# A streaming-encoder layer with a gathered expert stage on one core: the opening's fillers cut into single products, half of tile 1's top-64 moved among the first dots, tile 1's first attention steps moved four picks later

## The reference

```python
h = rmsnorm(x, ln1_g)
q_a, k_a, v_a, q_i, k_i, w_i, q_b, k_b, v_b, g_b = project(h, w_in)
dots = einsum('bthd,bsd->bths', q_i, k_i)                       # indexer
score = einsum('bth,bths->bts', w_i, relu(dots))
top_s, idx = lax.top_k(score, topk)                              # 64 of the prompt's keys
p = softmax(q . k_sel[idx] * 64 ** -0.5); o_a = p @ v_sel[idx]   # sparse attention, 8 heads
o_b, S = retention_mix(q_b, k_b, v_b, g_b, ...)                  # chunked retention, 4 heads
x = x + concat([o_a, o_b]) @ w_out
h2 = rmsnorm(x, ln2_g)                                           # then the experts:
q = h2 @ w_query; s1, s2 = q . keys1, q . keys2                  # 8 heads, 2 halves, 128 keys each
e_idx, gate = top 16 of the 16 x 16 sums of the two top-16s, softmax
x = x + sum_k gate_k * gelu(exp_u[e_idx_k] . h2) * exp_v[e_idx_k]
y = rmsnorm_final(x)
```

## Time and profile before

| | |
|---|---|
| median of 3 runs | 1145.2 us (1144.81 to 1145.22) |
| profiled execution: time, span | 1146.64 us, 1144.6 us |
| PE, PEld busy | 865.9 us (76%), 398.9 us (35%) |
| DVE, ACT, POOL busy | 784.9 us (69%), 453.8 us (40%), 538.3 us (47%) |
| DMA | 456.58 MB, 399 GB/s mean over the span |

### The profile page before, as it was taken

The page is one execution under the profiler, slowest core; times in us unless marked ns, Lnnn a source line. Parts: engine busy times, 40 slices in busy tenths (PEclk is TensorE's granted clock), DMA queues, the critical chain, the costliest instruction groups (busy, mean ns, idle before and its releaser), DMA issues.

```text
span 1144.6 us, 12068 instructions
## 1 busy us (share of the span) xinstructions
PE 865.9 (76%) x3879; PEld 398.9 (35%) x3884; DVE 784.9 (69%) x2005; ACT 453.8 (40%) x1423; POOL 538.3 (47%) x437
## 2 busy tenths in 40 slices
PE   8999989997896958684687677677676666666556
PEld 6748754443232424241233342233223222211111
DVE  2325877866677888896666785857877777667554
ACT  2121444433444334543554663343433333333334
POOL 0002536553555555563543454555564555556442
PEclk9999989999999888897888999698888889977788
DMA  9902999999999999999999999999999999999996
GB/s 375 410 2 70 415 427 424 426 426 429 425 427 426 426 428 420 411 410 406 426 428 424 425 426 428 405 427 426 426 428 426 426 427 426 427 427 427 426 428 265
DMA packets 66790, 456.58 MB, mean 399 GB/s; under 512 B 8227, under 2 KB 10019, under 8 KB 15526
## 3 DMA queue, kind: packets, MB, share of 16 engines
q0 software_dynamic: 55888, 402.68, 83.9%
q1 hardware_dynamic: 10694, 52.87, 11.3%
q10 hardware_dynamic: 144, 0.26, 0.1%
HBM read 451.49 MB, written 3.24 MB: 397 GB/s over the span
## 4 chain that ended last, share of the span: by engine, by line
DMA 47%; PE 28%; DVE 9%; POOL 6%; ACT 5%; issue 4%; SPq 0%; POOLq 0%; DVEq 0%
DMA rows<-in_uv,ids 38%; PE ps L598 28%; DMA wt<-in_uv,ids 6%; DVE rows L2043 5%; POOL rows L537 4%; POOL work L520 2%; ACT wt L1249 2%; ACT work L1249 1%; DMA rows<-in_w_qi 1%; DMA wt<-in_uv,last_ids 1%; ACT wgt L1249 1%; DMA wt<-in_w_q 1%; PE ps L601 1%; ACT L1249 1%; DVE wt L2043 1%
## 5 line engine op out<-in xcount | busy, mean ns | idle before, releaser
L537 POOL DMA_INDIRECT rows<-in_uv,ids x352 | 399.1, 1134 | 442.1 <-PE ps L598 357.4
L598 PE MATMUL ps<-rows,work 128*64 128x512 f32 x1416 | 416.5, 718 | 239.1 <-ACT work L1249 236.1
L2043 DVE CUSTOM_DVE_ANT_0 rows<-rows,wt 128x1024 f32<-128x1024 f32 x226 | 276.6, 1224 | 164.7 <-DMA rows<-in_uv,ids 160.7
L1249 ACT ACTIVATE zact<-zdot 128x1 f32<-128x1 f32 x354 | 71.5, 202 | 489.7 <-DVE zdot L2043 483.1
L598 PEld LDWEIGHTS ps<-rows,work 128*64 128x64 f32 x1416 | 97.1, 153 | 476.4 <-ACT work L1249 329.4
L598 PE MATMUL ps<-wt 128*128 128x128 f32 (+6 forms) x719 | 195.2, 473 | 26.0 <-ACT wt L1249 24.2
L2043 DVE CUSTOM_DVE_ANT_0 rows<-rows,masks 128x1024 f32<-128x1024 f32 x128 | 157.1, 1229 | 67.5 <-DMA rows<-in_uv,ids 63.0
L598 PEld LDWEIGHTS ps<-wt 128*128 128x128 f32 (+2 forms) x724 | 98.4, 187 | 102.4 <-issue 59.1
L1249 ACT ACTIVATE work<-pair,wgt 128x64 f32<-128x64 f32 x354 | 123.1, 348 | 11.5
L1249 ACT ACTIVATE wgt<-zact,gates 128x1 f32<-128x1 f32 x354 | 104.3, 295 | 11.5
L598 PEld LDWEIGHTS ps<-work,wt 128*128 128x128 f32 (+1 forms) x664 | 83.6, 201 | 47.3 <-issue 46.9
(11 more groups left out here) (178 smaller groups left out, 727.4 us busy)
## 6 DMA issues: line engine op xcount, KB each, us to landing
wt<-in_w_q SPq DMA_DIRECT2D x7, 2048.0 KB, 15.9
rows<-in_uv,ids POOLq DMA_INDIRECT x352
rows<-in_w_out SPq DMA_DIRECT2D x2, 2048.0 KB, 32.4
wt<-in_w_out SPq DMA_DIRECT2D x2, 2048.0 KB, 11.3
wt<-in_ckv SPq DMA_DIRECT2D x16, 256.0 KB, 12.0
x<-in_x SPq DMA_DIRECT2D x5, 512.0 KB, 9.0
rows<-in_w_qi SPq DMA_DIRECT2D x1, 2048.0 KB, 13.5
wt<-in_w_qa SPq DMA_DIRECT2D x1, 2048.0 KB, 12.8
```

What stands on the lines that cost most here:

```text
L537: pool.indirect_dma_start(row[s], None, a["uv"], bass.IndirectOffsetOnAxis(ap=ids[:, own(n // KP).start + n % KP:own(n // KP).start + n % ...
L598: return nc.tensor.matmul(out, lhsT, rhs, start=start, stop=stop)
L1249: return nc.scalar.activation(*args, **kw)
L2043: V.tensor_tensor_reduce(row[s][:, 0:D], row[s][:, 0:D], h2r[t][:, n % 2, :], 1.0, 0.0, ALU.mult, ALU.add, zdots[s]).then_inc(dotted, 1)
```

## The change

It does four things. (1) `index_queries` counts single products instead of groups of eight, so the fillers around `query(0)` and its scores are cut finer, and the transposes of h2 are made in two halves (`h2_t0`), each when its half of h2 is there; the wait for the square, whose scratch lies in h2T, goes to the two engines that copy. (2) `spread_out(0)` stands after `sums_1(0)`, ahead of `dots_1(3)` and `sums_1(1)`. (3) `y_start(0)`, which starts y with x, comes at tick 12 and adds; `add_experts(0)` starts the sum instead. (4) VectorE makes four of tile 1's eight rounds ahead of dot 0 and the others after dots 0 to 3, and tile 1's scores, maxima, exponentials, transposes and values come two to six ticks later, with `exps_1(0)` and `exps_1(1)` in two ticks instead of one; three projections follow. Left out of the diff: renumbered calls for tile 0, and the waits and places of the projections and of `retention_1`.

```diff
@@ -627,12 +627,12 @@
-            def index_queries(t, bank, j0, j1):
-
-                for j in range(j0, j1):
-                    for c in range(KC):
-                        last = mm(ps[:, bank, j * P:(j + 1) * P], w_qi[:, c, j * P:(j + 1) * P], hT(t, c), c == 0, c == KC - 1)
-                if j1 == 4:
+            def index_queries(t, bank, i0, i1):
+
+                for i in range(i0, i1):
+                    j, c = divmod(i, KC)
+                    last = mm(ps[:, bank, j * P:(j + 1) * P], w_qi[:, c, j * P:(j + 1) * P], hT(t, c), c == 0, c == KC - 1)
+                if i1 == 4 * KC:
                     last.then_inc(qi_ps, 1)
...
@@ -786,12 +786,15 @@
+            def h2_t0(e):
+                pe.wait_ge(gained, e + 1)
+                for c in range(4 * e, 4 * e + 4):
+                    last = tr(ps[:, 3 * e, (c % 4) * P:(c % 4 + 1) * P], h2[:, c * P:(c + 1) * P])
+                if e:
+                    last.then_inc(h2t_ps, 1)
+
             def h2_t(t):
-                if t == 0:
-                    pe.wait_ge(gained, 2)
-                    pe.wait_ge(sqd, H2_STAT[0] + 1)
-                else:
-                    pe.wait_ge(hready, TILES + t + 1)
+                pe.wait_ge(hready, TILES + t + 1)
                 if t == 1:
...
@@ -864,7 +867,7 @@
                 for e in range(2):
-                    last = mm(ps[:, Y_BANK[t] + e, :], ident[:], x[:, t, e * 512:(e + 1) * 512], True, False)
+                    last = mm(ps[:, Y_BANK[t] + e, :], ident[:], x[:, t, e * 512:(e + 1) * 512], t > 0, False)
                 last.then_inc(y_init, 1)
...
@@ -878,39 +881,39 @@
-                        last = mm(ps[64 * j:64 * j + 64, Y_BANK[n // (HP * KP)] + e, :], diag[s], row[s][:, D + e * 512:D + (e + 1) * 512], False, stop)
+                        last = mm(ps[64 * j:64 * j + 64, Y_BANK[n // (HP * KP)] + e, :], diag[s], row[s][:, D + e * 512:D + (e + 1) * 512], n == 0, stop)
                 last.then_inc(acc, 1)
...
             mm(ps[:, 2, 0:P], e8[64:64 + HI, :], kiw[64:64 + HI, P:2 * P]).then_inc(w_ps, 1)
-            index_queries(1, 6, 0, 1)
-            h2_t(0)
-            index_queries(1, 6, 1, 2)
+            h2_t0(0)
+            index_queries(1, 6, 0, 3)
+            h2_t0(1)
+            index_queries(1, 6, 3, 7)
             query(0)
-            index_queries(1, 6, 2, 3)
+            index_queries(1, 6, 7, 9)
             query_scores(0)
-            index_queries(1, 6, 3, 4)
+            index_queries(1, 6, 9, 32)
             pe.wait_ge(gb_sb, 1)
-            index_queries(2, 7, 0, 1)
+            index_queries(2, 7, 0, 4)
             pe.wait_ge(qi_sb, 2)
             pe.wait_ge(wz_set, 2)
             dots_1(0)
             dots_1(1)
             dots_1(2)
             sums_1(0)
+            spread_out(0)
             dots_1(3)
             sums_1(1)
-            spread_out(0)
             sums_1(2)
             sums_1(3)
-            index_queries(2, 7, 1, 4)
+            index_queries(2, 7, 4, 32)
             query(1)
             later_qa(0)
             query_scores(1)
             pe.wait_ge(qi_sb, 3)
-            y_start(0)
             add_experts(0)
             later_qa(1)
             add_experts(2)
...
@@ -940,7 +943,7 @@
-            PROJECTIONS = ((14, "qkb", 1, 3), (24, "vb", 1, 3), (30, "vb", 2, 2),
+            PROJECTIONS = ((18, "qkb", 1, 3), (26, "vb", 1, 3), (32, "vb", 2, 2),
                            (36, "gb", 1, 3), (42, "qkb", 2, 2), (48, "gb", 2, 3))
...
@@ -1143,15 +1146,18 @@
             def attention_1():
+                yield from until(6)
                 scores_1(0)
-                yield from until(6)
+                yield from until(8)
                 scores_1(1)
-                yield from until(14)
+                yield from until(12)
+                y_start(0)
+                yield from until(18)
                 prob_t1(0)
-                yield from until(18)
+                yield from until(22)
                 values_1(0)
                 prob_t1(1)
-                yield from until(22)
+                yield from until(26)
                 values_1(1)
...
@@ -1309,6 +1315,8 @@
 
             def h2_take(t):
                 act.wait_ge(h2t_ps, t + 1)
+                if t == 0:
+                    act.wait_ge(sqd, H2_STAT[0] + 1)
...
@@ -1435,17 +1443,18 @@
             def background():
-                yield from until(11)
+                yield from until(15)
                 exps_1(0)
+                yield
                 exps_1(1)
-                yield from until(19)
+                yield from until(22)
                 prob_t1(0)
-                yield from until(22)
+                yield from until(25)
                 values_1(0)
                 prob_t1(1)
-                yield from until(25)
+                yield from until(28)
                 values_1(1)
-                yield from until(29)
+                yield from until(31)
                 act.wait_ge(rt_ps, 2)
                 copy(rT1, bank4(0)).then_inc(rt_sb, 1)
...
@@ -1716,6 +1725,8 @@
             def h2_take(t):
                 dve.wait_ge(h2t_ps, t + 1)
+                if t == 0:
+                    dve.wait_ge(sqd, H2_STAT[0] + 1)
...
@@ -1870,10 +1881,9 @@
-            for r in range(0, TOPK[1], 8):
+            for r in range(0, TOPK[1] // 2, 8):
                 whole(score_round(score1, r, TOPK[1], 0))
                 whole(score_round(score1, r, TOPK[1], 1))
-            set_bias(bias1, score1)
...
@@ -1895,16 +1905,20 @@
             def attention_1():
-                yield from until(8)
+                for r in range(TOPK[1] // 2, TOPK[1], 8):
+                    whole(score_round(score1, r, TOPK[1], 0))
+                    yield from score_round(score1, r, TOPK[1], 1)
+                set_bias(bias1, score1)
+                yield from until(12)
                 yield from row_max(1, [ps[:, b, :].rearrange("p (j n) -> p j n", j=2) for b in (1, 2)], 0, 4)
-                yield from until(10)
+                yield from until(14)
                 yield from row_max(2, [ps[:, b, :].rearrange("p (j n) -> p j n", j=2) for b in (0, 3)], 4, 4)
-                yield from until(15)
+                yield from until(18)
                 yield from scale_probs(1, prob1[:, 0, :, :], 0, 4)
                 yield from scale_probs(2, prob1[:, 1, :, :], 4, 4)
 
             def retention_1():
-                yield from until(23)
+                yield from until(25)
                 dve.wait_ge(cs_again, 16)
```

More of the change, by code:

```diff
@@ L646, in _ @@
             pe.wait_ge(w_in["qi"], 16)
-            index_queries(0, 4, 0, 2)
+            index_queries(0, 4, 0, 16)
             norm_t(1)
-            index_queries(0, 4, 2, 3)
+            index_queries(0, 4, 16, 24)
             norm_t(2)
-            index_queries(0, 4, 3, 4)
+            index_queries(0, 4, 24, 32)
             keys_values(1)
@@ L950, in projections @@
                     w, s = {"qkb": (w_qkb, qk_ps), "vb": (w_vb, vb_ps), "gb": (w_gb, gb_ps)}[name]
-                    if start == 14:
+                    if start == 18:
                         pe.wait_ge(expd, 3)
-                    if start == 24:
+                    if start == 26:
                         pe.wait_ge(rotated, 2)
-                    if start == 30:
+                    if start == 32:
                         pe.wait_ge(pv_sb, 3)
@@ L986, in retention_1 @@
             def retention_1():
-                yield from until(26)
+                yield from until(28)
                 pe.wait_ge(rotated, 2)
@@ L1384, in natural @@
             def natural():
-                for start, dst, t, bank, s, done, func in ((33, vb, 1, 3, vb_ps, vb_sb, ACT.Copy), (39, vb, 2, 2, vb_ps, vb_sb, ACT.Copy),
+                for start, dst, t, bank, s, done, func in ((34, vb, 1, 3, vb_ps, vb_sb, ACT.Copy), (39, vb, 2, 2, vb_ps, vb_sb, ACT.Copy),
                                                            (45, gs, 1, 3, gb_ps, gb_sb, ACT.Silu), (57, gs, 2, 3, gb_ps, gb_sb, ACT.Silu)):
```

## The result

| | before | changed |
|---|---|---|
| median of 11 runs each | 1144.81 us (1143.93 to 1145.42) | 1148.77 us (1147.34 to 1151.97) |
| profiled execution: time, span | 1146.64, 1144.6 us | 1147.89, 1145.9 us |

The ratio is 1.004, 95% interval 1.0032 to 1.0048: 4 us slower, where 1143.0 was forecast and the range ended at 1145.3. The two profiled executions lie only 1.3 us apart: before's lies above all eleven of its timed runs, and moved 411 GB/s in 440 to 544 where the changed kernel's moved 426 (3.7 us over these 104 us).

The account below looks back on a forecast made before the run. The prediction took the DMA stream, busy at 426 GB/s from 172 to 440, as the bound. Gather 0 earlier (-2.3) and a dip at w_q's load (+0.1) gave -2.2 us, hence 1143.0 us, range 1142.0 to 1145.3.

Parts of the forecast that it names:

- The opening and the spread: Start of the kernel up to the first gather: finer fillers and an earlier spread bring gather 0 2.3 us earlier, at 107.57.
- TensorE's pace decides: Rival, behind gather 0: the queue runs dry and TensorE, only 1.1 us ahead, sets the time, 1144.1 us; 2 in 10.
- the dip that was charged 0.1: DMA queue near 140, when w_q is loaded: margin only 0.1 us, so 0.1 charged, between 0 and 0.5 for the range.
- Behind the load: After w_q's load: TensorE pauses about 1 us, query(2) starts about 147 and may take 3.74, gather 20 goes about 161.
- The price of part 4: Tile 1's moved rounds and exponentials: about 8.8 us of idle TensorE before add_experts(16), gather 24 at about 176.8, cost 0.
- The drain of 1.38 us for each switch: Rule against the forecast, at ScalarE's four table switches: gather 24 another 5.5 us later, 2.7 beyond the spare, 1145.7 us.
- 2.8 us to spare, cost 0: DMA queue at gather 24: 4.4 us queued against a lag of 1.6, so the idle TensorE costs nothing.
- From there picks come at the stream's pace.: Everything behind gather 24: no further loss was counted there.
- The one that ends slower: Rival: the hole at picks 15 to 17 empties the queue, gather 24 after 184, typically 1147.8 us; 13 in 100.
- The check I had named: If gather 0 is earlier but the end isn't: look for DMA windows under 1.0 between 137 and 185.
- More than forecast: Rival: ScalarE's copy is hidden, gather 0 comes 2.7 us earlier and the ledger has slack, 1142.4 us; 1 in 10.

Follow-up runs that it names:

- e6: Changed kernel without its earlier opening and with the spread in its old place: 1150.81 us, ratio 1.0054 to the kernel before.
- e10: e5 without the opening and with the spread in its old place: 1145.61 us, ratio 1.0002 to the kernel before.
- e4: Kernel before with only the opening and the earlier spread of the change: 1144.52 us, ratio 0.9994.
- e9: e2 with each group of four exponentials made twice, so the pause before add_experts(16) is 12.85 us: 1149.36 us, ratio 1.0032.
- e2: Changed kernel with the qkb projection of tile 1 at TensorE's ticks 16 to 20 instead of 18 to 22: 1144.41 us, ratio 0.9993.
- e5: Changed kernel with both groups of exponentials in one ScalarE tick and the qkb projection at 16 to 20: 1143.15 us, ratio 0.9987.
- e1: Changed kernel with tile 1's exponentials in one ScalarE tick again, two table loads instead of four: 1146.28 us, ratio 1.0009.
- e3: Changed kernel with the exponentials in one ScalarE tick and the qkb projection started at tick 14: 1143.67 us, ratio 0.9983.
- e8: Changed kernel with rotate(1) at VectorE's tick 27 instead of 25 and its users two ticks later: 1150.28 us, ratio 1.0050.
- e7: Kernel before with the qkb projection at TensorE's ticks 18 to 22 instead of 14 to 18: 1158.01 us, ratio 1.0113.
- e13: Kernel before with the qkb projection started at tick 16 instead of 14: 1146.54 us, ratio 1.0011.
- e12: Changed kernel with three of eight products left out of the two vb projections, output no longer the reference's: 1149.15 us, ratio 1.0032.

## Why the prediction was wrong, by its own steps

**The opening and the spread: mechanism right, size off.** All places came within 0.7 us. Their value was put at the full 2.3 us of an earlier gather 0, less 0.1. e6 and e10 measure 1.6 and 1.7 us (give or take 1.8 and 1.4 by the intervals), e4 0.7 on the kernel before, with an interval that reaches past none. Part of where it goes is in the windows: e4 has 354, 352 and 342 GB/s from 128 to 140 and had by 172 moved 26.22 MB, exactly as much as the kernel before. The rival "TensorE's pace decides" holds there in full. In the changed kernel it holds in small: w_q was issued at 138.58 (forecast 139.17), and the dip that was charged 0.1 is this row:

```profile
140.00:144.00 4.00, 3.52 (x24) 1.48 (x24) 3.75 (x9) 3.22 (x13) 2.76 (x2) 1.00 0.93 369
```

4 us at 369 instead of 426 GB/s: 0.5 us, the upper end of the bound.

**Behind the load: right.** `query(2)` at 147.63 after 1.13 us of pause, 3.81 long; gather 20 at 161.17.

**The price of part 4: place right, conclusion wrong.** ScalarE's four table loads and two groups of exponentials, and `add_experts(16)` at 173.58 after 8.91 us of idle TensorE (173.6, 8.8), came as summed; gather 24 at 177.55 (176.8). The chain around the first two loads:

```profile
162.61 1.28 ACT L1255
...
163.90 1.93 ACT wt L1255 x8
...
165.85 1.28 ACT L1255
```

The load takes 1.28 us and the exponentials start 0.01 us behind it, as in the earlier trace rows. The drain of 1.38 us for each switch, which the Trainium skill gives in "ScalarE: Activation LUTs", "What ACT_TABLE_LOAD costs", isn't seen here either.

"2.8 us to spare, cost 0" was right for gather 24 (e9: about 2.4). The step that failed is the next sentence: "**From there picks come at the stream's pace.**" I had checked the queue at the one gather behind the pause and then let the engines run freely. What the runs showed in its place: TensorE leaves the pause late against VectorE, which catches up by 191. The projection that `rotate(1)` needs had been moved from 14 to 18 on TensorE, its reader only from 23 to 25 on VectorE, so five ticks of distance became three. VectorE waits 4.65 us in front of dots that it could make, TensorE 2.97 for these, and gathers 32 to 36 go 2.6 to 5.5 us later than in the kernel before, with a stream that needs them 2.4 us earlier. With the projection two ticks earlier 5.4 us of it are gone (e2). I had both numbers of the table before me and priced only the exponentials of part 4, not the three projections that follow it.

**The rivals.** The one that ends slower had the right sign and a typical 1147.8, but another place: it wanted gather 24 after 184, from a late `query(2)` or a drain. Neither came. The check I had named, windows under 1.0 between 137 and 185, finds only the small one at 140 (176 to 180 has 0.98); the loss stands at 200 to 224, outside it. *More than forecast* had its condition met, gather 0 being 2.9 us earlier, and came out on the wrong side all the same: the place of gather 0 didn't decide the time.

**The sum with the measured terms** (differences of ratios, times 1145): opening and spread -1.7 us (e6, e10), the projection's distance +5.4 (changed kernel against e2), the pause by itself +0.7 (e2 against e5): 4.4, where 4.0 by the medians and 4.6 by the ratio were measured. That it closes says no more than that e10 lies within 0.2 us of the kernel before. How the last two terms share the 6.1 us depends on the order: with the pause shortened first (e1) it is worth 3.5 us, and the projection 2.5 (e1 against e5). The best versions, e3 and e5, are 1.9 and 1.5 us faster than the kernel before, where 2.2 were forecast: most of what the change was to give is there once the projection stands earlier and the exponentials in one tick.

**What stays open.** Why the opening is worth 1.7 and not 2.3 in e5 was followed only to 172 (by then e5 had moved 26.93 MB and e10 26.58, a lead of 0.8 us; by 260 it was 1.7). Why a stretch like 440 to 544 moves 411 to 416 GB/s in some executions and 423 to 426 in others wasn't tried.

## What to carry to other kernels

Where several in-order engines share one hand-made schedule, a table of places is a table of distances: for each product moved, note on the reader's engine how many ticks lie between its end and its use, before and after, and ask which engine will be ahead of the other at that time, not on average. But e8 had its five ticks and lost: the count is a place to look, and what counts is when the producer gets there. A pause that the queue covers is not over when the queue has held; it leaves one engine late against another, and the next wait between the two is where it is paid, here 25 us later. A product moved out of its place can also leave its engine idle there (e7, e13). Time in which the bounding resource has nothing queued was hardly bought back by less work behind it (e12), and a wait isn't cured by putting its reader later when the next instruction waits for the same engine (e8): put the producer earlier (e2).

## What the runs showed that I had not expected

Two ticks of one projection, 7.4 us of TensorE's work in all, moved the kernel by 5.4 us in one version and 1.3 in another, and four ticks by 13 us (e2, e13, e7). And TensorE's granted clock fell during the idle stretch and came back only behind it. The products ahead of it end at 164.7; the clock is 1.00 in 164 to 168, falls in the next window and is 0.50 in 172 to 176 (the lower of the two levels, 1.2 GHz against 2.4); TensorE works again from 173.58, first at that level, and has 1.00 again from 180:

```profile
168.00:172.00 4.00, 0.00 (x0) 0.00 (x0) 3.93 (x7) 3.95 (x11) 2.37 (x2) 0.56 1.06 449
172.00:176.00 4.00, 2.42 (x6) 0.77 (x8) 3.86 (x10) 2.93 (x10) 0.00 (x0) 0.50 0.99 422
176.00:180.00 4.00, 4.00 (x15) 1.14 (x12) 1.91 (x4) 1.06 (x5) 2.15 (x2) 0.66 0.98 416
180.00:184.00 4.00, 4.00 (x18) 1.94 (x18) 2.04 (x3) 2.44 (x7) 2.43 (x3) 1.00 1.01 424
```

The sixteen products of `add_experts(16)` and `add_experts(18)` took 6.20 us there, where eight take 1.94 in rows at a clock of 1.00, so this pause cost some 2.3 us more than its own length. Behind the 2.97 us of pause at 202.20 it is eight products in 3.29 us, with a clock of 0.83 in 200 to 204 and 0.74 in 204 to 208.
